# The gated delta projections as three products of rounded and rest parts, in a kernel of two model blocks on one NeuronCore

## The reference, cut to what matters

```python
h = rms_norm(x, g) * (1 + scale) + shift          # 256 context and 256 latent tokens, 1024 wide
p = h @ w_in                                       # columns 0..4095: q, k, v, z of 8 heads of 128
qkv = silu(conv(p[..., :3072]))                    # 3x3 on the latent grid, 3 taps on the context
q, k = l2_normalize(q), l2_normalize(k)
beta = sigmoid(p_beta); g = -exp(a_log) * softplus(p_a + dt_bias)
# per head and direction, in chunks:
m = strict_tril((k * beta) @ k.T * decay)
sol = triangular_solve(m + I, [v * beta, k * beta * exp(g)])
# then a scan over the chunks with a 128x128 state
y = rms_norm(o) * silu(z)
```

## Time and profile before

| | us |
|---|---|
| three runs before: lowest, median, highest | 3105.13, 3109.87, 3116.91 |
| the profiled execution, its own time | 3102.32 |
| its span | 3100.5 |
| busy PE / PEld / DVE / ACT / POOL | 2899.1 / 2391.6 / 2130.6 / 1609.0 / 143.3 |

### The profile page before, as it was taken

One profiled execution on the slowest core, in us unless ns is written; L12 is line 12 of the kernel. 1 busy time (PEld: TensorE's weight loads), 2 busy tenths in 40 slices (PEclk: granted clock), 3 DMA queues, 4 the chain that ended last, 5 costly groups with the idle time before them and its releaser, 6 DMA issues. The chain is left out here.

```text
span 3100.5 us, 43235 instructions
## 1 busy us (share of the span) xinstructions
PE 2899.1 (94%) x16872; PEld 2391.6 (77%) x16873; DVE 2130.6 (69%) x3242; ACT 1609.0 (52%) x2237; POOL 143.3 (5%) x175
## 2 busy tenths in 40 slices
PE   5899999979999999999999999998887999988998
PEld 2678888857679877777777777776875999976998
DVE  3154555537746789999999999997574565574675
ACT  0243544412206378878788788785432445432453
POOL 0123222200000000000000000000000000000000
PEclk9799999989969899999999999999985899985999
DMA  4531110044306699999999999994630355530553
GB/s 151 102 73 48 28 28 1 1 152 131 100 1 202 199 376 381 378 378 384 381 375 385 381 376 385 379 386 163 206 99 1 114 173 175 142 98 1 159 183 122
DMA packets 257974, 604.60 MB, mean 195 GB/s; under 512 B 26114, under 2 KB 82665, under 8 KB 257385
## 3 DMA queue, kind: packets, MB, share of 16 engines
q1 hardware_dynamic: 256684, 601.35, 56.1%
q10 hardware_dynamic: 1085, 0.45, 0.1%
HBM read 596.29 MB, written 5.44 MB: 194 GB/s over the span
## 5 line engine op out<-in xcount | busy, mean ns | idle before, releaser
L2277 DVE TENSOR_TENSOR moe_raw_r<-moe_raw,moe_hi 128x2048 fp32r<-128x2048 f32 x320 | 718.9, 2283 | 7.6 <-ACT moe_hi L2480 7.6
L2480 ACT ACTIVATE moe_hi<-moe_raw 128x2048 fp32r<-128x2048 f32 x320 | 599.9, 1907 | 8.4 <-PE banks L2364 4.3
L2820 PE MATMUL banks<-xs_r,w_hi 128*128 128x272 f32 (+1 forms) x1632 | 474.5, 291 | 28.7 <-DVE w_raw_r L3242 20.0
L2824 PE MATMUL banks<-xs_r,w_raw_r 128*128 128x272 f32 (+1 forms) x1632 | 472.0, 289 | 0.0
L2821 PE MATMUL banks<-xs_r,w_hi 128*128 128x272 f32 (+1 forms) x1632 | 469.6, 288 | 0.0
L3064 ACT ACTIVATE w_hi<-w_raw 128x512 fp32r<-128x512 f32 (+1 forms) x416 | 256.8, 619 | 245.5 <-PE banks L2824 200.8
L2820 PEld LDWEIGHTS banks<-xs_r,w_hi 128*128 128x128 f32 x1632 | 310.7, 190 | 33.8 <-issue 25.8
L2824 PEld LDWEIGHTS banks<-xs_r,w_raw_r 128*128 128x128 f32 x1632 | 310.6, 190 | 3.0
L2821 PEld LDWEIGHTS banks<-xs_r,w_hi 128*128 128x128 f32 x1632 | 311.1, 191 | 0.2
L3242 DVE TENSOR_TENSOR w_raw_r<-w_raw,w_hi 128x512 fp32r<-128x512 f32 (+1 forms) x416 | 271.2, 674 | 58.0 <-ACT w_hi L3064 54.0
L2403 PEld LDWEIGHTS banks<-con,gu_tok 128*128 128x128 f32 x1024 | 191.1, 192 | 29.2 <-ACT gu_tok L2492 9.6
(11 more groups left out here) (490 smaller groups left out, 5476.1 us busy)
## 6 DMA issues: line engine op xcount, KB each, us to landing
moe_raw<-in_w_gu SPq DMA_DIRECT2D x256, 1024.0 KB, 8.2
moe_raw<-in_w_down SPq DMA_DIRECT2D x128, 1024.0 KB, 10.2
w_raw<-in_w_ff SPq DMA_DIRECT2D x256, 256.0 KB, 3.0
w_raw<-in_w_in SPq DMA_DIRECT2D x112, 256.0 KB, 2.7
wq<-in_w_in SPq DMA_DIRECT2D x32, 512.0 KB, 4.4
mod_ring<-in_w_mod SPq DMA_DIRECT2D x16, 1024.0 KB, 5.9
ring_mod<-in_w_mod SPq DMA_DIRECT2D x4, 2048.0 KB, 20.1
wh<-in_w_in SPq DMA_DIRECT2D x8, 1024.0 KB, 9.5
```

Source lines behind the costliest of these rows:

```text
L2277: dve.tensor_tensor(rest[n % UNITS][:, :], raw[n % UNITS][:, :], hi[n % HI_SLOTS][:, :].bitcast(F32), ALU.subtract).then_inc(los, 1)
L2480: act.activation(hi[n % HI_SLOTS][:, :], raw[n % UNITS][:, :], ACT.Copy).then_inc(his, 1)
L2820: pe.matmul(bank, w_hi, x[:, 0, 0:n_cols], start=first, stop=False)
L2824: ins = pe.matmul(bank, w_lo, x[:, 0, 0:n_cols], start=False, stop=last)
```

## The change

1. **Projections.** `project` takes three products: rounded weights with rounded tokens, rounded weights with the tokens' rest, and the weights' rest with rounded tokens. The rounded weights lie in a ring of three slots (`w_hi`), the rest overwrites the loaded weights in place (`w_lo` is the memory of `w_raw`), so that the weights of the next head are loaded once a projection is through. `w_round` on ACT and `w_rest` on DVE make the parts, 128x1024 at a time, for head s+2: ACT rounds in levels 3, 4, 5 and behind `k_out`, DVE subtracts in levels 4, 5, 6 behind the taps and behind the scaling of `osb`.
2. **Tokens.** `hT_hi` and `hT_lo` are made in the stage of the gates; `hT_lo` lies in the memory of `hT`. In the levels of the last head DVE adds the two back for the stages behind.
3. **Gates' stage.** Head 0's four projections run in it, with its evacuations and its 33 taps (`first_taps`, one tensor after the other), and the block over the heads starts at s = -1.
4. **Preparation.** One stage in place of two. PE waits for the first 16 small transfers alone, sums the squares before the groups of `w_mod`, and takes these in the order 2, 3, 0, 1; `shifted` of the first four tiles runs before the last group's rows are turned. All loads of the gates' stage and of head 0 are issued here.

```diff
+        def w_round(act, h, n):
+            u = 4 * h + n
+            act.wait_ge(loaded[n], 16 * (h + 1))
+            if u >= W_HI:
+                act.wait_ge((k_mm, v_mm, q_mm, z_mm)[(u - W_HI) % 4], (u - W_HI) // 4 + 1)
+            act.activation(w_hi[:, u % W_HI, :, :], w_raw[:, n, :, :], ACT.Copy).then_inc(w_hi_a, 1)
+
+        def w_rest(dve, h, n):
+            u = 4 * h + n
+            dve.wait_ge(w_hi_a, u + 1)
+            dve.tensor_tensor(w_lo[:, n, :, :], w_raw[:, n, :, :], w_hi[:, u % W_HI, :, :], ALU.subtract).then_inc(w_lo_v, 1)
+
+        def project(pe, h, n, out, lo, ks):
+            u = 4 * h + n
+            for k in ks:
+                if k == 0:
+                    pe.wait_ge(w_lo_v, u + 1)
+                if u == 0:
+                    pe.wait_ge(h_lo_v, k + 1)
+                hi = w_hi[:, u % W_HI, k, :]
+                pe.matmul(out, hi, hT_hi[:, k, lo:TOK], start=(k == 0), stop=False)
+                pe.matmul(out, hi, hT_lo[:, k, lo:TOK], start=False, stop=False)
+                ins = pe.matmul(out, w_lo[:, n, k, :], hT_hi[:, k, lo:TOK], start=False, stop=(k == KT - 1))
+            return ins
-                        ins = pe.matmul(out, wq[:, h % 2, n, k, :], hT[:, k, lo:TOK], start=(k == 0), stop=(k == KT - 1))
...
-                        sp.wait_ge(used, h - 1)
-                        load(sp, h, n)
+                        sp.wait_ge(used, h)
+                        first.load(sp, a, h, n)
...
+                            if 3 <= lv <= 5 and live(s + 2):
+                                w_round(act, s + 2, lv - 3)
...
+                            if lv >= 4 and live(s + 2):
+                                w_rest(dve, s + 2, lv - 4)
+                            if s == H - 1:
+                                dve.wait_ge(z_mm, H)
+                                for k in ((lv,) if lv < LEVELS - 1 else range(lv, KT)):
+                                    dve.tensor_tensor(hT[:, k, :], hT_lo[:, k, :], hT_hi[:, k, :], ALU.add)
...
                     if live(s - 1):
-                        dve.tensor_tensor(osc[:, :, :], osb[:, :, :], nrin[:, 6:8].unsqueeze(2).broadcast_to([P, 2, P]),
+                        dve.tensor_tensor(osb[:, :, :], osb[:, :, :], nrin[:, 6:8].unsqueeze(2).broadcast_to([P, 2, P]),
                                           ALU.mult).then_inc(on_v, 1)
+                    if live(s + 2):
+                        w_rest(dve, s + 2, 3)
```

The stage of the gates, on PE and DVE:

```diff
                 ins.then_inc(mm, 1)
+                project(pe, 0, 0, ps[6][:, :], 0, range(KT)).then_inc(k_mm, 1)
                 pe.wait_ge(on_dve, 8)
...
+                    if i == 4:
+                        pe.wait_ge(k_in, 1)
+                        project(pe, 0, 1, ps[6][:, :], 0, range(KT)).then_inc(v_mm, 1)
+                    if i == 8:
+                        pe.wait_ge(v_in, 1)
+                        project(pe, 0, 2, ps[6][:, 0:LAT], CTX, range(KT)).then_inc(q_mm, 1)
+                        project(pe, 0, 3, ps[6][:, LAT:TOK], CTX, range(KT)).then_inc(z_mm, 1)
...
                 for i in range(1, H2, 2):
                     dve.wait_ge(rows, i + 1)
-                    dve.tensor_copy(grow[:, i % 2 * H + i // 2, :], ps[4 + i % 4][:, :]).then_inc(row_dve, 1)
+                    dve.tensor_copy(grow[:, i % 2 * H + i // 2, :], ps[BANK[i % 4]][:, :]).then_inc(row_dve, 1)
+                    if i == 3:
+                        w_rest(dve, 0, 3)
+                    if i == 3 or i == 7:
+                        first_taps(dve, c, i // 4)
...
                 dve.tensor_copy(metaT[:, :, :], ps[2][:, 0:KT * META].rearrange("p (k t) -> p k t", k=KT))
+                first_taps(dve, c, 2)
...
-                for s in range(-2, H + 1):
+                for s in range(-1, H + 1):
```

The preparation, on DVE behind the group of squares:

```diff
+                group(0)
+                group(1)
+                group_out(0)
+                group(2)
+                group_out(1)
...
+                group(3)
+                group_out(2)
...
+                for k in range(4):
                     shifted(k)
+                group_out(3)
+                dve.wait_ge(taken, 4)
+                for k in range(4, KT):
+                    shifted(k)
```

More of the change, by code:

```diff
@@ L431, in _ @@
                 for g, r, src in rows:
[L432 to L445, removed]
-                for k in range(KT):
[L447 to L468, removed]
-                sp.dma_start(wba[:, :, :], a["w_in"][0, :, COL_BETA:COL_BETA + 32].rearrange("(k p) n -> p k n", p=P)).then_inc(wba_in, 16)
-            @block.gpsimd
-            def _(pool):
-                pool.tensor_copy(xT[:, :, :], allT[:, :, CTX:TOK]).then_inc(latent, 1)
-            @block.scalar
-            def _(act):
-                act.activation(cs[:, :, :], vec[:, V_C:V_C + 16].rearrange("p (s k) -> p k s", s=2), ACT.Silu).then_inc(cs_in, 1)
-                for k in range(KT):
+                    act.dma_start(stg[r:r + src.shape[0], g, :], src).then_inc(rows_in if g < 2 else late_in, 16)
@@ new lines, in _ @@
+                    if g == 1 and r == 16:
+                        for half in range(2):
+                            act.dma_start(stg[20:22, 1, half * 64:half * 64 + 64], a["diff_norm_2"]).then_inc(rows_in, 16)
+                act.wait_ge(rows_v, 2)
+                act.activation(cs[:, :, :], vec[:, V_C:V_C + 16].rearrange("p (s k) -> p k s", s=2), ACT.Silu).then_inc(cs_in, 1)
+                act.preload_act_table(ACT.Sqrt)
+                for k in range(KT):
+                    act.wait_ge(tok_v, k + 1)
@@ new lines, in _ @@
+                pe.wait_ge(rows_v, 2)
+                for k in range(KT):
+                    pe.wait_ge(squared, k + 1)
+                    ins = pe.matmul(ps[0][:, :], ones, sq[:, k, :], start=(k == 0), stop=(k == KT - 1))
+                ins.then_inc(norm_sum, 1)
+                pe.wait_ge(late_in, 16 * sum(g >= 2 for g, _, _ in rows))
+                pe.wait_ge(tok_v, KT)
+                for g in range(2, 8):
+                    bank = ps[1] if g >= 4 else ps[6]
+                    ins = pe.transpose(bank[:, g % 4 * P:g % 4 * P + used[g]], stg[:used[g], g, :], ident[:used[g], :used[g]])
@@ L499, in _ @@
                     ins.then_inc(summed, 1)
[L500 to L506 removed]
+                    if j == 1:
+                        pe.wait_ge(late_v, 6)
+                    if j:
+                        turn(j - 1)
@@ L602, in gdn @@
         osb = sb("osb", [P, 2, P])
-        osc = sb("osc", [P, 2, P])
-        junk = sb("gjunk", [P, 8, P])
         nsum = sb("nsum", [P, 8])
```

559 lines of the change are left out of this document (323 added, 236 removed).

## The result

The changed kernel takes 3057.32 us in the median of four runs (3053.48 to 3069.14), the kernel before 3107.50 (3104.45 to 3116.91). The ratio is 0.985, 95% interval 0.9826 to 0.9874. The profiled execution takes 3057.30, against 3102.32 before: 45.0 less, where the sum of the prediction said 44; for the median it said 3062, and 3044 to 3082 as the range. A second set of runs of the same kernel gave 0.9872 (0.9843 to 0.99).

What follows compares the result with a forecast made beforehand. The prediction took PE to bound the heads' turns, nearly without gaps. Its terms, 16 (loop) + 13 (preparation) + 15 (gates, heads 0 and 1) = 44 us, took 3102.3 to 3058, 3062 for a median; range 3044 to 3082.

Steps and rivals of the forecast that it cites:

- The loop: Heads 2 to 7: shorter projections on PE gain 3.7 us a head gross, 2.7 net, 16 us for six heads.
- 0.5 for level 4: Levels of a head: DVE's first rest makes the next copy 0.7 late, idling PE 0.5 us a head, between 0 and 2.9.
- 0.5 for the chain: Chain of states: V's shorter products cover less of it, so of V's 1.28 us gain 0.8 is kept.
- rival B: Levels: DVE becomes the bound; with rests of 2.4 us the heads gain nothing, 3078 us; chance 0.14.
- rival D: Turns: new PE idle time lowers the granted clock; a quarter turn at half clock eats 44 us; chance 0.03.
- The preparation: Front before the gates' stage: an earlier start and a shorter stage gain 13 us, bounds 8 and 17.
- The start: PE's first transpose, waiting for 16 small transfers instead of 20, comes at 15 instead of 17.95; 2.5 us taken as gain.
- then half of L524, 2.6: End of the preparation: only half of the token shifting, 2.6 us, stands behind the last group.
- Gates, heads 0 and 1: From the gates' start to head 0's inversion: 90 us instead of 105.6, gain 15, bounds 4 and 24.
- the 28 us for the block's first turn: Block behind the gates' stage: 14 us until V starts, POOL's tables taking 8.5, then 14 to head 0's inversion.
- rival C: Front: small transfers land at 18, gates' stage at low clock, POOL's tables slowed; gains 8 + 4 instead of 28, 3078 us; chance 0.09.
- E: Projections over 256 columns: an fp32r product costs 0.144, so Q and Z gain nothing, 9 us lost, 3071 us; chance 0.01.

Runs made afterwards that it cites:

- x_shares: Changed kernel with the next head's 33 taps shared over the levels as (3, 6, 6, 6, 4, 4, 4) instead of (1, 6, 6, 6, 6, 5, 3); 3064.45 us.
- x_wait20: Changed kernel with PE waiting before its first transpose for 20 small transfers instead of 16; 3075.16 us.
- x_groups: Changed kernel with the modulation groups taken in order 0, 1, 2, 3 again and the tokens shifted behind the last group; 3059.99 us.
- x_qtaps: Changed kernel with head 0's nine Q taps moved from the gates' stage into the block behind it, after head 1's three rests; 3065.28 us.
- x_float32: Changed kernel with each projection again one float32 product, without the rests and the additions restoring hT; median 3075.17 us, ratio 0.9897 to the kernel before.
- x_best: Changed kernel with four edits: Q's taps between the rests, head 0's tables earlier, osb transposes behind Q's projection, taps reshared; median 3061.60 us, ratio 0.9858.
- x_pool: Changed kernel with POOL's twelve table operations for head 0 moved from the block into the gates' stage; 3065.14 us.
- x_twice: Changed kernel with the weight subtractions of levels 4 and 5 done twice in heads 2 to 7; 3061.27 us.
- x_two_b: Changed kernel leaving the product with the tokens' rest out of the projections from head 2 on; 3028.64 us.
- x_osb: Changed kernel with the two transposes of osb moved behind Q's projection; 3064.63 us.

## Why the prediction was right, step by step

**The loop.** Right. Gross 3.7 a turn: K 1.24, Q and Z about 0.6 each and V 1.2 without its wait are 3.6. Taken back: I had 0.5 for level 4, and x_shares gives 0.5 (its record 0.29); I had 0.5 for the chain, and the wait for `S` (0.6 in the starts) and the 0.35 before Q come to nearly twice that. This is the term that was mis-sized. The net is 2.3 a turn in turns two to six and 3.3 in the first, 14.85 in six, against 16. Of the causes I had named one, the scaling beside POOL: it is the 0.35 before Q. The larger one I had not seen. DVE's three small steps for the variance (L1215 to L1218) stand ahead of the update of `S`:

```profile
317.83 0.73 DVE L1215 TENSOR_SCALAR nstd<-nsum 128x2 f32<-128x2 f32 x1
...
318.54 1.02 DVE L1218 TENSOR_SCALAR nstd<-nsum 128x4 f32<-128x4 f32 x1
319.48 0.59 DVE L1206 SCALAR_TENSOR_TENSOR S<-S,gates,banks 128x128 f32<-128x128 f32 x2
```

They stood there before the change too (1.3 us from the first to the update, now 1.65), and V's longer products covered them. No edit moved them: this cause is read from the order of the rows. In the first turn there is no head before: L1215 and the scaling fall away, the other two take 0.16 each, PE waits for neither, and the turn gains 1.0 more:

```profile
200.18 0.16 DVE L1218 TENSOR_SCALAR nstd<-nsum 128x4 f32<-128x4 f32 x1
```

Why L1218 takes 1.02 in one turn and 0.16 in another is open. The fourth rest is slow beside POOL's kbg and kd, as osc was: the line's durations (lowest, median, highest ns), of which 2068 is the fourth rest of the turn shown:

```profile
L702 DVE TENSOR_TENSOR gdn_w_r<-gdn_w,gdn_w_hi x32: 1212/1224/2068, 64.7 to 503.5; 128x1024 fp32r<-128x1024 f32 x32
```

The estimate of 1.2 holds for the rests in the levels, and with it rival B is refuted. It does not hold for all: from head 1 on the fourth rest, seven of 32, takes 1.96 to 2.07, over the 1.5 that the prediction gave as a sign of being wrong. It lies behind the scaling and not in a level, and PE has no wait for it in the turns.

**"A turn of about 44 where it was 47"** was a mistake of mine: 47 us was the window that I had cut for the earlier trace rows, while the turn was 61.74. The sum didn't use it; rival D's 44 us did, whose price was so too small, and the clock stayed at 1.00 in the turns.

**The preparation.** Gain 15.3, forecast 13 (8 to 17). The start was sized too small: 6.05 instead of 2.5. I took landing to follow issue by 8 us as it did for the last transfer; the last of the sixteen were issued from 6.23 on and had landed at 11.9, under 6 behind, while with all of them PE waits until 17.47 (x_wait20). The shorter stage was sized too large: 9.3 instead of 10.5. From PE's first transpose to the end of `shifted` it took 50.0 where the sum has 49.2, and the meeting behind it 1.75 where it was 1.3. The failed step in the sum is "then half of L524, 2.6": both halves, 5.3, stand behind the last group (56.44 to 61.89; x_groups). Most of these 2.7 is made up, since the copy and the turning of the last group run beside the first half instead of before it, and the late transposes took 0.7 instead of 1.3.

**Gates, heads 0 and 1.** Gain 12.0, forecast 15 (4 to 24). The stage with its meeting took 61.9 from L804 to the block's start, forecast 61.7, and what ends it was right, Q's taps (x_qtaps). The failed step is the 28 us for the block's first turn: it took 31.7 (30.2 to 31.7 in the six executions of this front). POOL's tables last 10.8 for twelve where 8.5 was said, because DVE's rests run beside them (1.01 us a table, 0.69 without them in x_float32), then PE has idled 3.95 before L1011 and does part of V at half clock. I had this as part of rival C, at the right cause and too low a chance for a piece of it.

**What was luck.** That the whole, 45.0, comes so near to 44 is in part luck. The three terms, 16, 13 and 15, came out as 14.85, 15.3 and 12.0, together 42.2 against 44, with a term too small against two too large. The other 2.8 lie between head 6's inversion and the end, where the prediction had nothing and where executions of the changed kernel's versions differ by as much among themselves.

**The rivals.** C failed in its main part, the small transfers at 18. E failed: 0.12 at 256 columns. D did not occur in the turns. The rule of the Trainium skill (FP8 and Floating Point Precision, TensorE Precision Notes) of four passes for true FP32 would, as an estimate, have given 5.2 gross a turn; the measured 3.6 is the rows' pace, not the rule's.

## What to carry to other kernels

Cost a product's new form by the spacing of the same form elsewhere in the same trace: it held here to about 0.1 us a turn (3.7 against 3.6). Then ask, for every copy or rounding put on an engine's queue, what stands behind it there. When a front is shortened, look for the load that until then had just been in time: 2 us of slack ate 8 of 10.8 us gained.

## What was not expected of the hardware

The changed kernel's nine runs fall in two groups: 3053.5 to 3057.3 (five, mean clock 0.932 to 0.934) and 3068.0 to 3070.0 (four, 0.928). All four runs of x_best are at 0.928: 3061.6 lies 6 to 8 under the upper group and 4 to 8 over the lower. Stretches (in the columns of the earlier trace rows) of the changed kernel and of x_qtaps show where it comes from, in the same part of the program:

```profile
700.00:800.00 100.00, 97.67 (x441) 69.87 (x441) 77.83 (x140) 25.80 (x40) 0.00 (x0) 1.00 0.33 106
```

```profile
700.00:800.00 100.00, 97.67 (x404) 70.50 (x403) 69.40 (x128) 24.11 (x39) 0.00 (x0) 0.90 0.30 95
...
720.00:730.00 10.00, 8.84 (x34) 5.83 (x34) 6.49 (x14) 1.67 (x2) 0.00 (x0) 0.86 0.58 159
730.00:740.00 10.00, 10.00 (x29) 6.20 (x29) 5.17 (x11) 4.33 (x4) 0.00 (x0) 0.80 0.77 262
```

PE is busy in both for 97.67 of 100 us; in one the granted clock holds 1.00 (2.4 GHz), in the other it is 0.90 over the stretch and 0.86 and 0.80 in two slices of 10 us, and 441 products become 404. In those two slices the changed kernel's PE is as busy (8.84 and 10.00) at 1.00.

From GLA's start to the end, which no edit touches, it takes 2447.3 to 2447.8 us in the kernel before, in the changed kernel's two executions and in x_groups, and 2458.0 to 2458.9 in x_shares, x_qtaps, x_pool and x_wait20. But these are not two values alone: x_twice has 2444.8, x_two_b 2453.3, x_osb 2454.2, x_best 2455.6 and x_float32 2462.8. The stretch varies by 18 us from one execution to the next, more than any single term of the prediction. The prediction's sign for failing as a whole, another length behind 645 us, could therefore not be read from one pair of executions. What decides the length is open; whether an edit of the front can bring it about was not tried.
